# Index scores from stacked queries on the full array, in a two-block transformer program on one core

## The chip, the cores and the metric

One core of a Trainium2 chip runs the whole program in one launch. The metric is the device time of an execution in microseconds; the kernel before has a median of 1530.33 us over 3 runs (1530.08 to 1531.02).

## The reference

Two blocks of a transformer on 512 rows of width 1024, float32 throughout. The first block has three attentions side by side (a sparse one, A; a stick-breaking one, B; one over 256 memory rows, C), a gated merge and a feed-forward layer; the second block has an mLSTM layer and a dilated attention. What the change touches is the indexer of the sparse attention, which picks 128 keys for each query:

```
s     = einsum('bqhd,bkd->bqhk', iq, ik) * IDX_DIM ** -0.5     # 8 heads of 64, one shared key of 64
score = einsum('bqh,bqhk->bqk', iw, relu(s))                    # weighted sum over heads
score = where(key_chunk <= query_chunk, score, -inf)            # chunks of 64
_, idx = top_k(score, 128)
```

Queries 0 to 127 can only see 128 keys, so scores are needed for the query tiles 1 to 3 alone, against 256, 384 and 512 keys.

## The kernel before

Each engine has an instruction stream written out by hand; semaphores order them. Nearly all products run in a rounded float32 type (float32r) that loses low bits, so every operand is kept as a high part (rounded) and a low part (value less high part), and a product is made of three: high x low, low x high, high x high.

Weights come in numbered slabs of 2048 words a partition through two slots: SyncE loads a slab, ScalarE copies its high part (`split_hi`), GpSimd subtracts its low part, TensorE multiplies, and ScalarE and VectorE empty the two banks of the accumulator (PSUM) that belong to the slot.

The change lies in the stage that runs memory attention (C) in 20 steps. In each step TensorE does, in this order: the logits of one unit (head and query tile), the transposes of a unit three steps back, the output of one four steps back, then, in the steps of `SCORE_STEPS`, one score block, and last some products of weight slabs (`products_beside`, with the plan `BESIDE_C`): the two slabs of index queries `iq` in steps 0 to 4 and 5 to 12, and the first slab of `aqk` in steps 13 to 19.

A score block j (`score_pairs`: 12 of them) is a pair of heads 2p and 2p+1 and a query tile t of 1 to 3, in the order t = 1, 2, 3 for p = 0 to 3. Blocks 0 to 5 stand in steps 6 to 11, blocks 6 to 11 in steps 14 to 19. A block writes the two banks from `score_bank(j)`, which are those that the query slabs were in: blocks 0 to 5 reuse the banks of the first slab, 6 to 11 those of the second. A block waits for ScalarE and VectorE to have emptied its query slab (`ev_a`, `ev_v`) and for both ReLUs of the block before (`x_relu`).

The index queries lie transposed, two heads in one tile: head 2p on partitions 0 to 63, head 2p+1 on 64 to 127, in `iq_hi` (written by ScalarE, `index_queries`, line 1850) and `iq_low` (written by VectorE, `index_queries_low`, line 2406). The one key lies twice, on both halves, in `ik_hi` (lines 1845 and 1846) and `ik_low` (2399 and 2400). A score product uses 64 rows of the array; the two heads of a block use the two halves of it in turn.

Behind a block ScalarE takes ReLUs (`index_relus`, line 1861, one step later) and VectorE adds them up with the head weights in `masks` (`index_sums`, lines 2421 and 2424, two steps later). Behind the whole stage TensorE multiplies the other `aqk` slabs and the `av` slabs, while VectorE selects the 128 largest scores (`select`, lines 2470 and 2472), with GpSimd's masks (line 751) behind that; then attention A begins.

A step of ScalarE in this stage: ReLUs of the last step's block, a copy of transposed probabilities (1783), the exponents of this step's unit (1776), now and then the high part of an attention output (1876), then a query slab that has been finished, then the split of the next weight slab (1683). A step of VectorE: sums of the block two steps back, the minimum of this step's logits (2435), the normalisation of the last step's unit (2355), now and then the low part of an output (2359), then a finished query slab.

In the trace all matrix products have the line of the helper `mm` (842), so they are told apart by the tiles they read.

Of the kernel before, what the change touches and what calls it, by code (L numbers as in the profile page):

```python
# [19 lines left out]
F32 = mybir.dt.float32  # L20
F32R = mybir.dt.float32r
ALU = mybir.AluOpType
ACT = mybir.ActivationFunctionType
# [3 lines left out]
P = 128  # L27
S = 512
# [30 lines left out]
BASE, EV_A, EV_V, COUNT = {}, {}, {}, dict(STAGES)  # L59
# [132 lines left out]
def score_bank(j):  # L192

    return 2 if j < 6 else 0
# [32 lines left out]
def _program(nc, A, ctx):  # L227
# [3 lines left out]
    def place(name, kib, words, dtype=F32, parts=P):  # L231
        return nc.alloc_sbuf_tensor_at(name, [parts, words], dtype, offset=SB0 + int(kib * 1024))

    def arena(name, kib, words, dtype=F32, parts=P):
        return place(name, ARENA + kib, words, dtype, parts)

    def sem(name):
        return ctx.enter_context(nc.semaphore(name))
# [53 lines left out]
    cqT = arena("cqT", 0, 4 * S)  # L292
    yc_hi, yc_lo = arena("yc_hi", 0, 4 * S, F32R), arena("yc_lo", 8, 4 * S, F32R)
    mkT, mv = arena("mkT", 64, 4 * N_MEM), arena("mv", 68, 2 * HALF)
    iq_hi, iq_low = arena("iq_hi", 16, 4 * S, F32R), place("iq_low", 0, 4 * S, F32R)
    ik_hi, ik_low = arena("ik_hi", 24, S, F32R), place("ik_low", 8, S, F32R)
    relu = arena("relu", 74, 4 * S)
    iw_row = arena("iw_row", 26, S, parts=8)
    masks, work = arena("masks", 48, PACK), arena("work", 53, PACK)
# [66 lines left out]
    banks = ctx.enter_context(nc.psum_tensor("banks", [P, 8, 512], F32))  # L366
# [17 lines left out]
    ev_a, ev_v = sem("emptied_by_scalar"), sem("emptied_by_vector")  # L384
# [7 lines left out]
    x_mm, x_relu, x_acc = sem("index_mm"), sem("index_relu"), sem("index_acc")  # L392
# [26 lines left out]
    dl_gap, dl_factor = sem("dilated_gaps"), sem("dilated_factors")  # L419
    dp_norm, dp_tr, dp_copied, dp_pv = (sem(n) for n in ("dilated_scaled", "dilated_transposed", "dilated_copied", "dilated_outputs"))  # L420
    z_first, z_first_sig = sem("first_head_gate"), sem("first_head_gate_sigmoid")
    iq_lo = sem("first_index_query_lo")
    seam_lo, rows_made = sem("seam_slab_lo_piece"), sem("projected_rows_gained")
    first_lo = sem("first_slabs_lo")
    out_done = sem("out_done")
# [414 lines left out]
    def _(pe):  # L840
        def mm(out, lhsT, rhs, start, stop, **kw):
            return pe.matmul(out, lhsT, rhs, start=start, stop=stop, **kw)  # L842
# [208 lines left out]
        slot = wait_slab("ik", 0, 0, 0)  # L1051
        hi, lo = (slot_of(w, slot, KD * IK_W).rearrange("p (k c) -> p k c", k=KD) for w in (w_hi, w_lo))
        for k in range(KD):
            ins = mm3(banks[0:IK_W, 2 * slot, :], hi[:, k], lo[:, k], h_hi[:, k * S:(k + 1) * S], h_lo[:, k * S:(k + 1) * S],
                      k == 0, k == KD - 1)
# [5 lines left out]
        for step in range(16 + LAG_OUT):  # L1061
            if step < 16:
                h, t = divmod(step, 4)
                attn_logits(U_C + step, lambda u: mm(banks[:, 4 + u % 2, 0:N_MEM], cqT[:, h * S + t * P:h * S + (t + 1) * P],
                                                     mkT[:, h * N_MEM:(h + 1) * N_MEM], True, True))
            if 0 <= step - LAG_T < 16:
                u = step - LAG_T
                attn_transposes(U_C + u, prob[(U_C + u) % 4], 2)
            if step >= LAG_OUT:
                u = step - LAG_OUT  # L1070
                h, t = divmod(u, 4)
                pe.wait_ge(at_trc, U_C + u + 1)
                if u == 0:
                    pe.wait_ge(iw_made, 1)
                if t == 0 and h >= 1:
                    pe.wait_ge(at_lo, h)
                for m in range(2):
                    ins = mm(banks[:, 7, t * P:(t + 1) * P], mv[:, m * HALF + h * P:m * HALF + (h + 1) * P],
                             probT[(U_C + u) % 2][:, m * P:(m + 1) * P], m == 0, m == 1)
                ins.then_inc(at_out, 1)  # L1080
            if step == 1:
                pe.wait_ge(ev_v, EV_V["ik"] + 1)
                for t in range(NT):
                    ins = pe.transpose(banks[:, 7, 8 * t:8 * t + 8], iw_row[:, t * P:(t + 1) * P], const("ident")[0:8, 0:8])
                ins.then_inc(iw_T, 1)
            for j, pair, t in score_pairs(step):
                pe.wait_ge(ev_a, EV_A["iq"] + 1 + pair // 2)
                pe.wait_ge(ev_v, EV_V["iq"] + 1 + pair // 2)
                if j:
                    pe.wait_ge(x_relu, 2 * j)  # L1090
                for n, (queries, keys) in enumerate(((iq_low, ik_hi), (iq_hi, ik_low), (iq_hi, ik_hi))):
                    for b in range(2):
                        rows = slice(64 * b, 64 * b + 64)
                        ins = mm(banks[:, score_bank(j) + b, 0:(t + 1) * P], queries[rows, pair * S + t * P:pair * S + (t + 1) * P],
                                 keys[rows, 0:(t + 1) * P], n == 0, n == 2)
                        if n == 2:
                            ins.then_inc(x_mm, 1)
            if step == 13:
                pe.wait_ge(x_relu, 12)
            products_beside(BESIDE_C, step)  # L1100
# [137 lines left out]
        for step in range(1, 8 + 2):  # L1238
# [17 lines left out]
            if step <= 8:  # L1256
                h = step - 1
# [155 lines left out]
        for step in range(1, 4 + 1):  # L1413
# [3 lines left out]
            if step >= 1:  # L1417
                h = step - 1
# [7 lines left out]
                for t in range(NT):  # L1426
                    if h:
                        pe.wait_ge(m_h, 4 * (h - 1) + t + 1)
                    for kt in range(t + 1):
                        off = TILE_AT[kt] + (t - kt) * P  # L1430
                        ins = mm(banks[:, 4 + t, 0:V1W], wts[h % 2][:, off:off + P], v1[:, (4 * kt + h) * V1W:(4 * kt + h + 1) * V1W], kt == 0, kt == t)
# [131 lines left out]
        for pair in range(4, 16):  # L1563
# [7 lines left out]
            if pair % 2:  # L1571
                n = pair // 2 - 2
# [84 lines left out]
    def _(act):  # L1657
# [189 lines left out]

        def index_queries(i, s, j, slot):
            for b in range(2):
                ins = act.activation(iq_hi[:, (2 * s + b) * S:(2 * s + b + 1) * S], banks[:, 2 * slot + b, :], ACT.Copy)  # L1850
            ins.then_inc(ev_a, 1)

        def index_relus(step):
# [12 lines left out]
        for step in range(16 + LAG_OUT):  # L1866
# [6 lines left out]
            if (step - LAG_OUT) % 4 == 3 and step >= LAG_OUT:  # L1873
                h = (step - LAG_OUT) // 4
# [19 lines left out]
        for step in range(32 + LAG_OUT):  # L1894
# [5 lines left out]
            if (step - LAG_OUT) % 8 == 7 and step >= LAG_OUT:  # L1900
                pair = (step - LAG_OUT) // 8
# [13 lines left out]
        for step in range(8 + 2):  # L1915
# [18 lines left out]
            for n, c in enumerate((LATER, FIRST)):  # L1934
# [3 lines left out]
                if 1 <= step <= 8:  # L1938
                    h = step - 1
# [7 lines left out]
            if step >= 3 and step % 2 == 1:  # L1947
                pair = (step - 3) // 2
# [145 lines left out]
        for step in range(4 + 2):  # L2094
            if step < 4:
                h = step
# [8 lines left out]
            if step >= 2:  # L2105
                h = step - 2
                if h:
                    act.wait_ge(m_ss, h)
                for t in range(NT):
                    act.wait_ge(m_h, 4 * h + t + 1)  # L2110
                    ins = act.activation(junk[:, 256 * t:256 * t + 256], o2[:, t * D + h * 256:t * D + (h + 1) * 256], ACT.Square,
                                         accum_out=head_ss[:, 4 * h + t:4 * h + t + 1])
# [153 lines left out]
    def _(dve):  # L2266
# [106 lines left out]
        for t in range(2):  # L2373
            ins = dve.tensor_scalar(root_diag[:, t * P:(t + 1) * P], const("ident"), root_of("mem", t), None, ALU.mult)
# [5 lines left out]
        keys = mkT[:].rearrange("p (h m) -> p h m", h=4)  # L2380
# [19 lines left out]
            dve.tensor_tensor(ik_low[64:128, :], banks[0:64, 2 * slot, :], ik_hi[0:64, :].bitcast(F32), ALU.subtract).then_inc(ev_v, 1)  # L2400

        def index_queries_low(i, s, j, slot):
            dve.wait_ge(ev_a, EV_A["iq"] + s + 1)
            for b in range(2):
                c = slice((2 * s + b) * S, (2 * s + b + 1) * S)
                ins = dve.tensor_tensor(iq_low[:, c], banks[:, 2 * slot + b, :], iq_hi[:, c].bitcast(F32), ALU.subtract)
            ins.then_inc(ev_v, 1)

        def score_row(t):
# [18 lines left out]
        for step in range(16 + LAG_OUT):  # L2428
# [10 lines left out]
            if (step - LAG_OUT) % 4 == 3 and step >= LAG_OUT:  # L2439
                h = (step - LAG_OUT) // 4  # L2440
# [12 lines left out]
        for t in range(1, NT):  # L2453
            diag = masks[:, ROW_AT[t] + t * P:ROW_AT[t] + (t + 1) * P]
            ins = dve.tensor_tensor(diag, diag, const("adm"), ALU.add)
# [21 lines left out]
        for n, (stage, s, empty) in enumerate(to_empty):  # L2477
# [3 lines left out]
            if n_now == n_select:  # L2481
                dve.wait_ge(selected, n_select)
                for t in range(1, NT):
                    ins = dve.tensor_scalar(score_row(t), work[:, ROW_AT[t]:ROW_AT[t] + (t + 1) * P], TAKEN, NEG, ALU.not_equal, ALU.mult)
# [12 lines left out]
        for step in range(32 + LAG_OUT):  # L2497
            if step < 32:
                u, t = U_A + step, head_and_tile(step)[1]
# [467 lines left out]
```

## Time and profile before

| | |
|---|---|
| median of 3 runs | 1530.33 us |
| the profiled execution | 1531.11 us, span 1529.4 us |
| TensorE products | 1508.4 us busy, 7624 instructions |
| TensorE weight loads | 1252.6 us busy |
| VectorE | 701.4 us busy |
| ScalarE | 604.4 us busy |
| GpSimd | 680.5 us busy |
| granted TensorE clock | 0.999 of full speed over the span |

The span is the time between the first and the last instruction that the profiler saw; the profiled execution's own time is 1.7 us longer. Busy times of TensorE count products that overlap, so a product's cost in a stream is the distance between starts. A row of a timeline can join several instructions of one kind (x2, x4).

### The profile page before, as it was taken

How to read it: one execution, taken by the hardware profiler on the slowest of the kernel's cores; microseconds unless marked ns; L12 is line 12 of the kernel's file. 1: busy time of each engine (PE TensorE's matmuls, PEld its weight loads, DVE VectorE, ACT ScalarE, POOL GpSimd, SP SyncE). 2: the span in 40 equal slices, each digit the busy share in tenths (PEclk: the TensorE clock that was granted, in tenths of full speed). 3: DMA queues.
4: the chain of work that ended last, by engine and by line, in shares of the span. 5: the costliest groups of instructions: out<-in, count | busy, mean ns of one | idle time of the engine just before them, and what ended most of it. 6: DMA issues, size and time to landing. Idle time of an engine off the chain costs nothing.

```text
span 1529.4 us, 19806 instructions
## 1 busy us (share of the span) xinstructions
PE 1508.4 (99%) x7624; PEld 1252.6 (82%) x7624; DVE 701.4 (46%) x1183; ACT 604.4 (40%) x925; POOL 680.5 (44%) x303
## 2 busy tenths in 40 slices
PE   7999999999999999999999999999999999999998
PEld 7877966977888888888888888888888888888887
DVE  3268955483224226666655004640026237355733
ACT  5353255574233225121212114522253443447552
POOL 6323465245555535444444344443442344445332
PEclk9999999999999999999999999999999999999999
DMA  7313312433433332433332324534421222333121
GB/s 240 113 55 123 99 56 70 120 87 111 130 103 102 98 109 75 115 100 95 97 102 91 110 83 56 114 89 105 120 87 49 97 83 83 103 109 106 50 90 56
DMA packets 152646, 148.42 MB, mean 97 GB/s; under 512 B 11088, under 2 KB 121680, under 8 KB 152444
## 3 DMA queue, kind: packets, MB, share of 16 engines
q1 hardware_dynamic: 147780, 139.24, 31.5%
q10 hardware_dynamic: 4792, 8.15, 1.6%
q8 instruction: 51, 0.84, 0.2%
q14 instruction: 23, 0.19, 0.0%
HBM read 137.87 MB, written 3.21 MB: 92 GB/s over the span
## 4 chain that ended last, share of the span: by engine, by line
PE 89%; issue 3%; ACT 3%; POOL 2%; DVE 2%; DMA 1%; ACTq 0%; SPq 0%; POOLq 0%; DVEq 0%
PE banks L842 86%; PE banks L871 2%; POOL w_lo L662 1%; PE banks L1030 1%; DMA sq<-in_c_sq 1%; POOL w_lo L682 1%; PE banks L1495 0%; ACT w_hi L1683 0%; POOL stick_a L723 0%; DMA vec_rows<-in_norm_a 0%; ACT k L2170 0%; ACT stick_a L1941 0%; ACT h_hi L1763 0%; DVE head_ms L2802 0%; POOL head_rs L805 0%
## 5 line engine op out<-in xcount | busy, mean ns | idle before, releaser
L662 POOL TENSOR_TENSOR w_lo<-raw,w_hi 128x2048 fp32r<-128x2048 f32 x103 | 476.8, 4629 | 579.0 <-ACT w_hi L1683 579.0
L842 PE MATMUL banks<-h_hi,w_hi 128*128 128x512 f32 (+1 forms) x904 | 350.1, 387 | 1.5 <-DVE h_lo L2340 0.8
L842 PE MATMUL banks<-h_hi,w_lo 128*128 128x512 f32 (+1 forms) x904 | 341.0, 377 | 0.0
L842 PE MATMUL banks<-h_lo,w_hi 128*128 128x512 f32 (+1 forms) x904 | 340.8, 377 | 0.0
L1683 ACT ACTIVATE w_hi<-raw 128x2048 fp32r<-128x2048 f32 (+2 forms) x123 | 233.2, 1896 | 206.4 <-PE banks L842 202.2
L842 PEld LDWEIGHTS banks<-h_hi,w_hi 128*128 128x128 f32 x904 | 170.2, 188 | 37.9 <-issue 5.8
L842 PE MATMUL banks<-w_hi,h_hi 128*128 128x512 f32 (+1 forms) x544 | 200.0, 368 | 0.0
L842 PE MATMUL banks<-w_hi,h_lo 128*128 128x512 f32 (+1 forms) x544 | 198.5, 365 | 0.0
L842 PE MATMUL banks<-w_lo,h_hi 128*128 128x512 f32 (+1 forms) x544 | 198.4, 365 | 0.0
L842 PEld LDWEIGHTS banks<-h_hi,w_lo 128*128 128x128 f32 x904 | 169.8, 188 | 32.0
L842 PEld LDWEIGHTS banks<-h_lo,w_hi 128*128 128x128 f32 x904 | 170.2, 188 | 28.8
L682 POOL TENSOR_TENSOR w_lo<-raw,w_hi 128x512 fp32r<-128x512 f32 x88 | 118.5, 1370 | 132.0 <-ACT w_hi L1683 119.7
L842 PEld LDWEIGHTS banks<-w_hi,h_hi 128*128 128x128 f32 x544 | 102.7, 189 | 16.2 <-issue 0.6
L842 PEld LDWEIGHTS banks<-w_hi,h_lo 128*128 128x128 f32 x544 | 102.7, 189 | 16.2
L842 PEld LDWEIGHTS banks<-w_lo,h_hi 128*128 128x128 f32 x544 | 102.7, 189 | 15.9
L2639 DVE TENSOR_TENSOR f_lo<-ff_prod,f_hi 128x512 f32 x22 | 104.3, 4741 | 2.7
L2026 ACT ACTIVATE ff_sig<-banks 128x512 f32<-128x512 f32 x22 | 13.2, 599 | 175.8 <-PE banks L842 175.8
L842 PE MATMUL banks<-w_hi,f_lo 128*128 128x512 f32 x176 | 68.6, 390 | 0.0
L842 PE MATMUL banks<-w_lo,f_hi 128*128 128x512 f32 x176 | 68.6, 390 | 0.0
L842 PE MATMUL banks<-w_hi,f_hi 128*128 128x512 f32 x176 | 68.6, 390 | 0.0
L1963 ACT ACTIVATE gate<-banks,col 128x512 f32<-128x512 f32 x23 | 15.8, 689 | 125.9 <-PE banks L842 125.9
L2322 DVE TENSOR_SCALAR meansq<-sumsq 128x1 f32<-128x1 f32 (+2 forms) x16 | 3.6, 228 | 134.9 <-ACT junk L1995 130.9
(355 smaller groups left out, 2320.2 us busy)
## 6 DMA issues: line engine op xcount, KB each, us to landing
raw<-in_w_in SPq DMA_DIRECT2D x56, 512.0 KB, 3.8
raw<-in_w_ffn_in SPq DMA_DIRECT2D x44, 512.0 KB, 4.9
raw<-in_w_in_a SPq DMA_DIRECT2D x32, 512.0 KB, 5.6
raw<-in_w_ffn_out SPq DMA_DIRECT2D x22, 512.0 KB, 4.0
raw<-in_w_ple_gate SPq DMA_DIRECT2D x16, 512.0 KB, 4.8
raw<-in_w_in_b SPq DMA_DIRECT2D x16, 512.0 KB, 4.5
raw<-in_w_out SPq DMA_DIRECT2D x8, 512.0 KB, 3.6
raw<-in_w_out_a SPq DMA_DIRECT2D x8, 512.0 KB, 4.4
```

The lines of the kernel that those rows point to most:

```text
L662: pool.tensor_tensor(slot_of(w_lo, slot), slot_of(raw, slot), slot_of(w_hi, slot).bitcast(F32), ALU.subtract).then_inc(lo_made, 1)
L682: ins = pool.tensor_tensor(w_lo[:, c], raw[:, c], w_hi[:, c].bitcast(F32), ALU.subtract)
L842: return pe.matmul(out, lhsT, rhs, start=start, stop=stop, **kw)
L871: ins = pe.transpose(banks[:, transposed_bank(name, k), t * P:(t + 1) * P], rows(t)[:, k * P:(k + 1) * P], const("ident"))
L1030: ins = pe.transpose(banks[:, 6, kt * P:(kt + 1) * P], src[:, kt * P:(kt + 1) * P], const("ident"))
L1683: act.activation(slot_of(w_hi, slot, words), slot_of(raw, slot, words), ACT.Copy).then_inc(hi_made, 1)
L1963: act.activation(gate[slot][:], banks[:, 2 * slot, :] if logits is None else logits, ACT.Sigmoid, bias=col[:, ds(V_BGATE + KD * (s % 3) + ...
L2026: act.activation(ff_sig[:], banks[:, 2 * slot, :], ACT.Sigmoid).then_inc(ev_a, 1)
L2322: dve.tensor_scalar(meansq[:, c], pieces[:, :, 0], EPS, None, ALU.add).then_inc(n_ms, 1)
L2639: dve.tensor_tensor(lo, ff_prod[:], hi.bitcast(F32), ALU.subtract).then_inc(lo_ffn, 1)
```

## The change

The queries of each head are stacked on 128 partitions in one tile, `iq_stack`: for an even head the high part on partitions 0 to 63 and the low part on 64 to 127, for an odd head the high part on 64 to 127 and the low part on 0 to 63. With the key's high part (or its low part) on both halves, one product over 128 rows gives (high + low) x key part, so a score is two full-array products, with `ik_low` and with `ik_hi`, and the product low x low is now in it.

ScalarE writes the high parts in four copies of 64 partitions a slab where it had two of 128, and signals after the first two; VectorE writes the low parts, each onto the other half of the partitions, in four subtractions where it had two, and starts on the first bank at that signal. `ik_low` moves to where `iq_hi` began.

```diff
--- before.py
+++ after.py
@@ -292,8 +292,7 @@
     cqT = arena("cqT", 0, 4 * S)
     yc_hi, yc_lo = arena("yc_hi", 0, 4 * S, F32R), arena("yc_lo", 8, 4 * S, F32R)
     mkT, mv = arena("mkT", 64, 4 * N_MEM), arena("mv", 68, 2 * HALF)
-    iq_hi, iq_low = arena("iq_hi", 16, 4 * S, F32R), place("iq_low", 0, 4 * S, F32R)
-    ik_hi, ik_low = arena("ik_hi", 24, S, F32R), place("ik_low", 8, S, F32R)
+    iq_stack, ik_hi, ik_low = place("iq_stack", 0, 8 * S, F32R), arena("ik_hi", 24, S, F32R), arena("ik_low", 16, S, F32R)
     relu = arena("relu", 74, 4 * S)
     iw_row = arena("iw_row", 26, S, parts=8)
     masks, work = arena("masks", 48, PACK), arena("work", 53, PACK)
@@ -419,7 +418,7 @@
     dl_gap, dl_factor = sem("dilated_gaps"), sem("dilated_factors")
     dp_norm, dp_tr, dp_copied, dp_pv = (sem(n) for n in ("dilated_scaled", "dilated_transposed", "dilated_copied", "dilated_outputs"))
     z_first, z_first_sig = sem("first_head_gate"), sem("first_head_gate_sigmoid")
-    iq_lo = sem("first_index_query_lo")
+    iq_lo, iq_first_hi = sem("first_index_query_lo"), sem("index_queries_first_hi")
     seam_lo, rows_made = sem("seam_slab_lo_piece"), sem("projected_rows_gained")
     first_lo = sem("first_slabs_lo")
     out_done = sem("out_done")
@@ -1088,13 +1087,10 @@
                 pe.wait_ge(ev_v, EV_V["iq"] + 1 + pair // 2)
                 if j:
                     pe.wait_ge(x_relu, 2 * j)
-                for n, (queries, keys) in enumerate(((iq_low, ik_hi), (iq_hi, ik_low), (iq_hi, ik_hi))):
-                    for b in range(2):
-                        rows = slice(64 * b, 64 * b + 64)
-                        ins = mm(banks[:, score_bank(j) + b, 0:(t + 1) * P], queries[rows, pair * S + t * P:pair * S + (t + 1) * P],
-                                 keys[rows, 0:(t + 1) * P], n == 0, n == 2)
-                        if n == 2:
-                            ins.then_inc(x_mm, 1)
+                for b in range(2):
+                    queries = iq_stack[:, (2 * pair + b) * S + t * P:(2 * pair + b) * S + (t + 1) * P]
+                    mm(banks[:, score_bank(j) + b, 0:(t + 1) * P], queries, ik_low[:, 0:(t + 1) * P], True, False)
+                    mm(banks[:, score_bank(j) + b, 0:(t + 1) * P], queries, ik_hi[:, 0:(t + 1) * P], False, True).then_inc(x_mm, 1)
             if step == 13:
                 pe.wait_ge(x_relu, 12)
             products_beside(BESIDE_C, step)
@@ -1847,7 +1843,11 @@
 
         def index_queries(i, s, j, slot):
             for b in range(2):
-                ins = act.activation(iq_hi[:, (2 * s + b) * S:(2 * s + b + 1) * S], banks[:, 2 * slot + b, :], ACT.Copy)
+                for r in range(2):
+                    h, rows = 4 * s + 2 * b + r, slice(64 * r, 64 * r + 64)
+                    ins = act.activation(iq_stack[rows, h * S:(h + 1) * S], banks[rows, 2 * slot + b, :], ACT.Copy)
+                if b == 0:
+                    ins.then_inc(iq_first_hi, 1)
             ins.then_inc(ev_a, 1)
 
         def index_relus(step):
@@ -2400,10 +2400,13 @@
             dve.tensor_tensor(ik_low[64:128, :], banks[0:64, 2 * slot, :], ik_hi[0:64, :].bitcast(F32), ALU.subtract).then_inc(ev_v, 1)
 
         def index_queries_low(i, s, j, slot):
-            dve.wait_ge(ev_a, EV_A["iq"] + s + 1)
+            dve.wait_ge(iq_first_hi, s + 1)
             for b in range(2):
-                c = slice((2 * s + b) * S, (2 * s + b + 1) * S)
-                ins = dve.tensor_tensor(iq_low[:, c], banks[:, 2 * slot + b, :], iq_hi[:, c].bitcast(F32), ALU.subtract)
+                if b:
+                    dve.wait_ge(ev_a, EV_A["iq"] + s + 1)
+                for r in range(2):
+                    c, rows, other = slice((4 * s + 2 * b + r) * S, (4 * s + 2 * b + r + 1) * S), slice(64 * r, 64 * r + 64), slice(64 - 64 * r, 128 - 64 * r)
+                    ins = dve.tensor_tensor(iq_stack[other, c], banks[rows, 2 * slot + b, :], iq_stack[rows, c].bitcast(F32), ALU.subtract)
             ins.then_inc(ev_v, 1)
 
         def score_row(t):
```

## Rows read from the trace of the kernel before

**Rows 1.** The page, part 1: busy us, share of the span, instructions of each engine.
```profile
PE 1508.4 (99%) x7624; PEld 1252.6 (82%) x7624; DVE 701.4 (46%) x1183; ACT 604.4 (40%) x925; POOL 680.5 (44%) x303
```

**Rows 2.** Chain that ended last, 72 to 135 us: start us, us, what.
```profile
86.31 0.10 DVE iq_low L2406
86.92 0.69 DVE iq_low L2406
87.61 0.14 issue
```

**Rows 3.** TensorE's timeline, memory attention's steps: start us, us, line, operation [idle before].
```profile
87.75 0.39 PE L842 MATMUL banks<-ik_hi,iq_low 64*128 64x256 f32 x2 [0.49 <-DVE iq_low L2406]
...
88.64 0.40 PE L842 MATMUL banks<-h_lo,w_hi 128*128 128x512 f32 x1
...
91.06 0.44 PE L842 MATMUL banks<-ik_hi,iq_low 64*128 64x384 f32 x2
...
97.50 0.61 PE L842 MATMUL banks<-probT,mv 128*128 128x128 f32 x4
...
98.26 0.28 PE L842 MATMUL banks<-ik_low,iq_hi 64*128 64x256 f32 x2
98.38 0.28 PE L842 MATMUL banks<-ik_hi,iq_hi 64*128 64x256 f32 x2
98.58 0.51 PE L842 MATMUL banks<-h_hi,w_hi 128*128 128x512 f32 x1
98.92 0.40 PE L842 MATMUL banks<-h_lo,w_hi 128*128 128x512 f32 x1
...
104.14 0.61 PE L842 MATMUL banks<-probT,mv 128*128 128x128 f32 x4
...
105.91 0.39 PE L842 MATMUL banks<-h_lo,w_hi 128*128 128x512 f32 x1
...
107.72 0.61 PE L842 MATMUL banks<-probT,mv 128*128 128x128 f32 x4
...
108.39 0.39 PE L842 MATMUL banks<-h_lo,w_hi 128*128 128x512 f32 x1
...
113.90 0.39 PE L842 MATMUL banks<-ik_hi,iq_low 64*128 64x256 f32 x2
```

**Rows 4.** TensorE's timeline: full-array products of 512, 256 columns, and stick-breaking's stacked ones.
```profile
121.34 0.39 PE L842 MATMUL banks<-h_lo,w_hi 128*128 128x512 f32 x1
121.57 0.40 PE L842 MATMUL banks<-h_hi,w_lo 128*128 128x512 f32 x1
...
171.06 0.28 PE L842 MATMUL banks<-w_hi,h_hi 128*128 128x256 f32 x1
171.18 0.28 PE L842 MATMUL banks<-w_lo,h_hi 128*128 128x256 f32 x1
...
299.97 1.44 PE L842 MATMUL banks<-stacked 128*128 128x384 f32 x8
301.24 0.86 PE L842 MATMUL banks<-sp_hi,sums_r 128*128 128x384 f32 x6
```

**Rows 5.** ScalarE's timeline: index keys, the first query slab, block 0's ReLUs.
```profile
69.07 0.59 ACT L1845 ACTIVATE ik_hi<-banks 64x512 fp32r<-64x512 f32 x1 [2.94 <-PE banks L842]
69.67 0.59 ACT L1846 ACTIVATE ik_hi<-banks 64x512 fp32r<-64x512 f32 x1
...
85.13 1.07 ACT L1850 ACTIVATE iq_hi<-banks 128x512 fp32r<-128x512 f32 x2
...
90.28 0.64 ACT L1861 ACTIVATE relu<-banks 128x256 f32<-128x256 f32 x2
```

**Rows 6.** VectorE's timeline: low parts of the index keys and the second query slab.
```profile
70.30 0.68 DVE L2399 TENSOR_TENSOR ik_low<-banks,ik_hi 64x512 fp32r<-64x512 f32 x1 [0.54 <-ACT ik_hi L1846]
70.99 0.68 DVE L2400 TENSOR_TENSOR ik_low<-banks,ik_hi 64x512 fp32r<-64x512 f32 x1
...
112.35 1.29 DVE L2406 TENSOR_TENSOR iq_low<-banks,iq_hi 128x512 fp32r<-128x512 f32 x2 [1.27 <-ACT iq_hi L1850]
```

**Rows 7.** VectorE's timeline: the copy of the last value slab.
```profile
187.82 0.69 DVE L2292 COPY av<-banks 128x512 f32<-128x512 f32 x1 [1.79 <-PE banks L842]
```

## The prediction

> **What bounds the kernel now.** Read the page's busy times first: TensorE is busy for 1508.4 of 1529.4 us [rows 1], so a change counts only by what it does to TensorE's stream. The change lies in the stage where memory attention's 20 steps run beside the index scores, from about 84 to 132 us. The chain of waits of that stretch comes next: it stays on TensorE nearly throughout, and leaves it only for the emptying of the first index-query slab, ScalarE's high parts and then VectorE's low parts; the second low part ends at 87.61 [rows 2], and the first score product starts at 87.75, where the row names that wait, 0.49 us [rows 3]. So two things set the end here: the TensorE time of the 12 score blocks (one for a pair of heads and a query tile), and the emptying of two query slabs, which blocks 0 and 6 await. Last come the timelines of the three engines, read for starts, not busy times: products overlap, and what one costs is the distance from its start to the next.
>
> **The change part by part. The score products.** Before, a block has three products for each of two heads, on 64 rows each; a row of the trace joins the two heads (x2). With 256 keys the second and third such row start 0.12 apart (98.26, 98.38), so both heads' products pass in the time of one [rows 3]. The whole price of a block is read by comparing steps. From the step's memory-attention output to the second slab product behind it: 97.50 to 98.92 = 1.42 us with 256 keys, 104.14 to 105.91 = 1.77 with 512, and 107.72 to 108.39 = 0.67 where there is no block [rows 3]. A block costs 0.75 and 1.10, and by interpolation 0.93 with 384 keys. The 0.12 (0.23 with 512, as [rows 4] have it) three times over is only 0.36 (0.69): some 0.39 to 0.41 us of a block is fixed, at its start and its end.
>
> After, a block has four products on the full array. Full-array products of this type start 0.12 apart with 256 columns (171.06, 171.18) and 0.23 with 512 (121.34, 121.57) [rows 4]; 384 is taken as 0.176, between them. The stick-breaking stage already has this form, two products of one stationary operand in a row into one bank, in all four widths: eight of them take 299.97 to 301.24 = 1.27 us, 2560 columns [rows 4], which the figures above reproduce to 0.08. A block becomes 0.48, 0.70 or 0.93: less by 0.27, 0.22 and 0.17. Blocks 2 to 5 together (512, 256, 384, 512 keys) gain 0.83, and 8 to 11 the same. Blocks 0, 1, 6 and 7 start behind a wait (below), where the start's fixed cost is mostly hidden: block 0 takes 87.75 to 88.64 = 0.89 to the second slab product [rows 3], after 0.48 + 0.08 + 0.23 = 0.79, so I take 0.10 for blocks 0 and 6 and 0.05 for 1 and 7.
>
> The Trainium skill, in TensorEngine Tiling (Array Packing), section Key Properties, speaks against the change: row tiles run independently and in parallel, so two 64-row products cost one, and three such pairs become four. By that alone the blocks would cost 4 x (0.12 + 0.176 + 0.23) = 2.1 us more. The same list says that a change of tiling mode drains the array; the trace bears out both, and here the fixed 0.39 us is larger than the extra product.
>
> **Emptying the query slabs.** ScalarE's two copies of 128x512 become four of 64x512, VectorE's two subtractions also four. Half the partitions don't halve the time: ScalarE's 64x512 copies take 0.59 us each, VectorE's subtractions 0.68 [rows 5, 6]. Their distance matters as much. Two 128-row subtractions start 0.61 apart (86.31, 86.92) and two copies take 1.07 together, but a pair whose second writes the other half of the partitions doesn't overlap: copies 0.60 apart (69.07, 69.67), subtractions 0.69 (70.30, 70.99) [rows 2, 5, 6]. In the new order every instruction changes halves against the one before it, so I take 0.60 and 0.69. Bounds: 0.48 and 0.61 below; above, no row shows a subtraction from the upper half to the lower, and I allow it as much as double.
>
> The Trainium skill has a rule for it, in VectorE: DVE Perf Modes, section Two Vector instructions with no wait between them: an instruction whose operand or output starts in another quarter of the partitions than the last one's is held until all earlier ones have finished. By it all four are held, in both directions, and the emptying is the 0.69 case; without it, the 0.61 case below.
>
> First slab: ScalarE starts at 85.13 [rows 5], has the first half done at 86.32, VectorE starts 0.11 later (the new signal lets it go on the first half) and ends at 86.43 + 4 x 0.69 = 89.19, no longer waiting for ScalarE, which ends at 87.5. With the 0.14 of before, block 0 starts at 89.33: TensorE is 1.58 us late, 1.48 after the block. Behind the subtractions VectorE has the next step's minimum, ScalarE behind that the exponents, a weight-slab copy, and then block 0's two ReLUs, which block 1 awaits. They ended at 90.92, just before block 1's 91.06 [rows 3, 5], and now move by 1.67 (the minimum too was overlapped and isn't now): block 1 starts at 92.72, 1.66 late, 1.61 behind it. Blocks 2 to 4 bring this to 0.95, block 5 to 0.78.
>
> Second slab: what ScalarE and VectorE have in front of it hangs on TensorE's step 11 and comes 0.88 late (0.95 less 0.07 of slack). The subtractions, 112.35 to 113.64 and 0.26 before block 6 at 113.90 [rows 3, 6], become 112.35 + 0.88 + 0.12 + 2.76 = 116.11; block 6 starts at 116.26, 2.36 late, 2.26 behind it; block 7, by the same ReLU path, is 2.49 late, 2.44 behind it; blocks 8 to 11 leave **1.6 us**.
>
> **What else moves.** TensorE's other waits in these steps, for the softmax, look a step or more (3 us) back and take the delay. The next queue to mind is VectorE's top-k selection, which runs unbroken behind this stage; it had finished 1.79 us before the copy of the last value slab [rows 7], and its start moves with TensorE's step 19, by about as much as TensorE itself, so it costs nothing; beyond 1.8 us more than TensorE's shift it would. No DMA is added or moved; what lies behind waits on TensorE and moves with it. Moving the tiles' places costs nothing.
>
> **The sum**: 1529.4 + 1.6 = 1531.0 us of span, 1532.7 with the 1.7 that lie around it in the profiled run (1531.11). That run is 0.8 above the median, so for the median: 1530.33 + 1.6 = 1531.9 us.
>
> **The rivals.** (a) The emptying overlaps as 128-row instructions do (0.48, 0.61). Then block 0 is 1.22 late, block 1 1.20, block 6 1.52, block 7 1.57, the end 0.7: 1531.0. For it: the rows of two 128-row instructions; against it: both pairs of 64-row ones. (b) The emptying stays hidden and TensorE's gain stands alone: 2 x 0.83 plus 0.3 to 1.0 for the four other blocks, 1527.7 to 1528.4. That needs 64-row instructions at half the price, which rows 5 and 6 deny. (c) Slower: the fixed 0.39 us isn't the change of array shape but stays with the start of a block, where TensorE's queue has its three waits for emptied slabs and ReLUs. Then the eight free blocks cost 0.12, 0.17 and 0.22 more instead of less, 1.5 us instead of -1.7: +4.7, 1535.0. It decides from about half of the fixed cost, +3.2. For it: the gap ahead of a block stands where those waits are; against it: a gap stands behind a block too, where there is no wait (98.38 to 98.58 is 0.20 for 0.12), and the stick-breaking products follow a wait with none. Subtractions twice as long from the upper half to the lower, two in a slab, would end at about the same, +4.4.
>
> **How the numbers follow.** Forecast 58%, (a) 20%, (b) 7%, (c) with the long subtractions 10%, 5% for what I don't see. A measurement of this kernel tells 0.2% (3.1 us) from no change. Forecast, (a) and (b) lie within it, but for the far end of (b): faster 3%, same 87%, slower 10%. The range reaches from inside (b) to the point where (c) decides: 1529.5 to 1533.7.
>
> **What would show it.** Right: copies 0.60 and subtractions 0.69 apart; block 0 near 89.3 and block 6 near 116.3, both behind VectorE, blocks 1 and 7 behind ReLUs; free blocks of 0.48, 0.70 and 0.93 us; the products behind the stage some 1.6 us later than before, and that shift unchanged to the end. Wrong: a gap ahead of the free blocks, a selection that ends after the value products, or a shift that grows behind 190 us.

## The result, and the profile after

The changed kernel takes 1533.46 us (median of 22 runs, 1531.77 to 1536.54) against 1531.00 of the kernel before on the same chip (22 runs, 1530.08 to 1533.08): a ratio of 1.0017 with an interval of 1.0011 to 1.0023, 2.5 us more. Measured once more beside other kernels it was 1532.98 (11 runs) against 1531.18, 1.0014 (1.0005 to 1.0023). Both lie within the 0.2% that the prediction calls no change, but both intervals lie above 1: the kernel became a little slower. The profiled execution took 1533.76 us, with a span of 1532.0; [rows 1] read now:

```profile
PE 1509.2 (99%) x7600; PEld 1255.2 (82%) x7600; DVE 705.8 (46%) x1187; ACT 608.1 (40%) x929; POOL 680.2 (44%) x303
```

TensorE has 24 instructions fewer and is busy for 0.8 us more: the first sign that something beside the products moved. To place it, take the tile view of the kernel before, of the change, and of the change profiled a second time. The columns after the count are the shortest, median and longest duration in ns, then the first and the last start in us. In each pair of lines the first is memory attention's logits, the second those of the next attention.

```profile
L842 PE MATMUL banks<-mkT,cqT x32: 377/378/382, 68.9 to 116.2; 128*128 128x256 f32 x32
L842 PE MATMUL banks<-aqkT x64: 271/482/694, 187.7 to 261.4; 64*128 64x128 f32 x16, 64*128 64x256 f32 x16, 64*128 64x384 f32 x16, 64*128 64x512 f32 x16
```

```profile
L841 PE MATMUL banks<-mkT,cqT x32: 377/377/628, 68.5 to 119.1; 128*128 128x256 f32 x32
L841 PE MATMUL banks<-aqkT x64: 272/481/693, 190.3 to 264.0; 64*128 64x128 f32 x16, 64*128 64x256 f32 x16, 64*128 64x384 f32 x16, 64*128 64x512 f32 x16
```

```profile
L841 PE MATMUL banks<-mkT,cqT x32: 377/377/382, 69.0 to 118.5; 128*128 128x256 f32 x32
L841 PE MATMUL banks<-aqkT x64: 272/481/693, 189.7 to 263.4; 64*128 64x128 f32 x16, 64*128 64x256 f32 x16, 64*128 64x384 f32 x16, 64*128 64x512 f32 x16
```

From the first memory-attention logits to the first logits of the next attention is 118.8 us before, 121.8 after, 120.7 in the second profile. This distance, called the stage below, holds the difference: from there to the end of the span it is 1341.7 us in all three (1529.4 - 187.7, 1532.0 - 190.3, 1531.5 - 189.7 = 1341.8). What lies ahead of the stage differs between executions whatever the kernel (68.1 to 70.9 us in those below), and is left out of it. So the change costs 1.9 us in one execution and 3.0 in another.

The chain of waits after, where the kernel before has two copies [rows 5] and two subtractions [rows 2] (start, us, what; a piece in the chain can be a part of an instruction):

```profile
84.85 0.48 ACT iq_stack L1848
85.34 0.60 ACT iq_stack L1848
86.04 0.69 DVE iq_stack L2409
86.73 0.49 DVE iq_stack L2409
87.44 0.68 DVE iq_stack L2409
88.14 0.71 DVE iq_stack L2409
```

The four subtractions start 0.69, 0.71 and 0.70 apart. The four copies of the first slab in ScalarE's timeline, less one duration of 0.60, start 0.60 apart in the mean; VectorE's subtractions of the second slab end at 116.85:

```profile
84.75 2.40 ACT L1848 ACTIVATE iq_stack<-banks 64x512 fp32r<-64x512 f32 x4
114.05 2.80 DVE L2409 TENSOR_TENSOR iq_stack<-banks,iq_stack 64x512 fp32r<-64x512 f32 x4 [1.38 <-ACT iq_stack L1848]
```

TensorE's timeline of the same profile (start, duration, operation; in brackets the idle time ahead and what ended it), where [rows 3] had 87.75 and 113.90:

```profile
88.98 0.36 PE L841 MATMUL banks<-ik_low,iq_stack 128*128 128x256 f32 x1 [2.10 <-DVE iq_stack L2409]
...
89.60 0.63 PE L841 MATMUL banks<-h_hi,w_hi 128*128 128x512 f32 x1
90.03 0.63 PE L841 MATMUL banks<-h_lo,w_hi 128*128 128x512 f32 x1
...
99.74 0.61 PE L841 MATMUL banks<-probT,mv 128*128 128x128 f32 x4
...
100.89 0.40 PE L841 MATMUL banks<-h_lo,w_hi 128*128 128x512 f32 x1
...
105.89 0.61 PE L841 MATMUL banks<-probT,mv 128*128 128x128 f32 x4
...
107.49 0.39 PE L841 MATMUL banks<-h_lo,w_hi 128*128 128x512 f32 x1
...
116.94 0.36 PE L841 MATMUL banks<-ik_low,iq_stack 128*128 128x256 f32 x1 [1.38 <-issue]
...
120.43 0.41 PE L841 MATMUL banks<-ik_low,iq_stack 128*128 128x384 f32 x1 [0.31 <-ACT relu L1861]
```

Three things are to be seen. Block 0 is held 2.10 us (0.49 before), block 6 1.38; its row names no releaser, but it starts 0.09 behind the second slab's subtractions. The free blocks, those that wait for nothing, are cheaper: output to second slab product is 100.89 - 99.74 = 1.15 us with 256 keys and 107.49 - 105.89 = 1.60 with 512, where [rows 3] had 1.42 and 1.77. And behind block 0's hold the slab products start 0.43 apart and last 0.63, where the same form elsewhere starts 0.23 apart and lasts 0.39: six of them cost some 1.2 us more. The windows of the two profiles of the change say why (PE, PEld, DVE, ACT and POOL busy, granted clock, DMA share, GB/s):

```profile
89.00:93.00 4.00, 4.00 (x13) 3.21 (x14) 0.81 (x4) 2.94 (x5) 1.19 (x1) 0.57 0.00 0
```

```profile
89.00:93.00 4.00, 3.25 (x19) 2.76 (x19) 2.20 (x9) 3.14 (x7) 0.66 (x1) 1.00 0.02 4
```

In the first the granted clock fell, from its level of 2.4 GHz to 1.2, for most of these 4 us; in the second, behind a hold of the same 2.10 us, it did not. Rows of the second profile:

```profile
89.50 0.36 PE L841 MATMUL banks<-ik_low,iq_stack 128*128 128x256 f32 x1 [2.10 <-DVE iq_stack L2409]
...
90.05 0.40 PE L841 MATMUL banks<-h_hi,w_hi 128*128 128x512 f32 x1
90.29 0.40 PE L841 MATMUL banks<-h_lo,w_hi 128*128 128x512 f32 x1
...
92.95 0.41 PE L841 MATMUL banks<-ik_low,iq_stack 128*128 128x384 f32 x1 [0.25 <-ACT relu L1861]
...
116.38 0.36 PE L841 MATMUL banks<-ik_low,iq_stack 128*128 128x256 f32 x1 [1.39 <-issue]
...
119.87 0.41 PE L841 MATMUL banks<-ik_low,iq_stack 128*128 128x384 f32 x1 [0.31 <-ACT relu L1861]
```

### The profile page after: what moved, and what is told of

It reads as the page before. It is cut to its first block, busy times and chain, and to the rows that moved or that the text cites. A ratio compares the mean times of both kernels' runs of the same rounds, so it can differ in the third digit from the quotient of the medians.

```text
span 1532.0 us, 19766 instructions
## 1 busy us (share of the span) xinstructions
PE 1509.2 (99%) x7600; PEld 1255.2 (82%) x7600; DVE 705.8 (46%) x1187; ACT 608.1 (40%) x929; POOL 680.2 (44%) x303
## 4 chain that ended last, share of the span: by engine, by line
PE 89%; ACT 3%; issue 3%; POOL 2%; DVE 2%; DMA 1%; ACTq 0%; SPq 0%; POOLq 0%; DVEq 0%
PE banks L841 85%; PE banks L870 2%; POOL w_lo L661 1%; PE banks L1029 1%; DMA sq<-in_c_sq 1%; POOL w_lo L681 1%; ACT w_hi L1679 0%; PE banks L1491 0%; DVE iq_stack L2409 0%; POOL stick_a L722 0%; DMA vec_rows<-in_norm_a 0%; ACT k L2170 0%; ACT stick_a L1941 0%; ACT h_hi L1759 0%; DVE head_ms L2805 0%
## 5 line engine op out<-in xcount | busy, mean ns | idle before, releaser
L681 POOL TENSOR_TENSOR w_lo<-raw,w_hi 128x512 fp32r<-128x512 f32 x88 | 118.8, 1372 | 136.0 <-ACT w_hi L1679 123.7
```

What stands on the lines that cost most here:

```text
L681: ins = pool.tensor_tensor(w_lo[:, c], raw[:, c], w_hi[:, c].bitcast(F32), ALU.subtract)
```

## The experiments

Twelve runs, eleven of them of a new kernel, all timed in five rounds. Theory 1 is the forecast's: the products gain 2 us and the emptying of the query slabs takes more than that. Theory 3, in some expectations, is that a fall of the clock costs nothing that isn't regained. The diffs are against the change unless said otherwise, and shortened: `...`, `first`, `second` and `all 128 rows` stand for longer expressions. Each time stands with its ratio to the kernel before on the same chip.

**old_products**: the new emptying, with the old three products of 64 rows.

```diff
-                for b in range(2):
-                    mm(..., iq_stack[all 128 rows], ik_low, True, False)
-                    mm(..., iq_stack[all 128 rows], ik_hi, False, True)
+                for n, keys in enumerate((ik_hi, ik_low, ik_hi)):
+                    for b in range(2):
+                        mm(..., iq_stack[64 * b:64 * b + 64], keys[64 * b:64 * b + 64], n == 0, n == 2)
```

> The new emptying alone: eight half-partition instructions a slab, but three products of 64 rows a head as before (the low parts of the queries are written and awaited, not multiplied). Theory 1 (the emptying of the query slabs holds TensorE at blocks 0 and 6, in the profile of the change for 2.1 and 1.4 us, and behind the longer hold the granted clock falls to 0.57 for some 4 us; the full-array products themselves gain about 2 us): slower than the change by about 2 us, 1535.3, that is 4.4 us over before; holds at blocks 0 and 6 as in the change, and a stretch of about 3 us at half clock behind the first. Theory 2 (the emptying is hidden, and it is the full-array products that cost): about as before, 1531 to 1531.5.

Measured 1535.69, 1.0028 (1.0018 to 1.0039); stage 122.4. The granted clock is 1.00 throughout the stage: the fall expected behind block 0's hold didn't come in this profile.

**old_emptying**: the new products, with two copies and two subtractions of 128 partitions, and VectorE waiting for both copies as before.

```diff
-                for r in range(2):
-                    ins = act.activation(iq_stack[rows, h], banks[rows, 2 * slot + b, :], ACT.Copy)
+                ins = act.activation(iq_stack[:, first], banks[:, 2 * slot + b, :], ACT.Copy)
...
-                for r in range(2):
-                    ins = dve.tensor_tensor(iq_stack[other, c], banks[rows, ...], iq_stack[rows, c], ALU.subtract)
+                ins = dve.tensor_tensor(iq_stack[:, second], banks[:, ...], iq_stack[:, first], ALU.subtract)
```

> The new products alone: the slabs are emptied by two 128-partition copies and two 128-partition subtractions as before, into the same stack tile (so the parts lie in the wrong places of the stack and the scores are not the reference's). Theory 1: the free blocks keep 0.48, 0.70 and 0.93 us, block 0 waits about as long as before (0.5 to 0.7 us), no fall of the clock, and the time is 1.7 to 2.3 us under before: 1528.7 to 1529.3. Theory 2: still 1 to 2.5 us over before.

Measured 1529.16, 0.9987 (0.9978 to 0.9996); stage 117.2. The score blocks' waits for an emptying on TensorE's timeline, first with the old products, then with the old emptying:

```profile
91.41 0.39 PE L841 MATMUL banks<-ik_hi,iq_stack 64*128 64x256 f32 x2 [2.10 <-DVE iq_stack L2413]
119.17 0.39 PE L841 MATMUL banks<-ik_hi,iq_stack 64*128 64x256 f32 x2 [1.38 <-issue]
```

```profile
86.99 0.35 PE L841 MATMUL banks<-ik_low,iq_stack 128*128 128x256 f32 x1 [0.48 <-DVE iq_stack L2403]
```

The two halves of the change add up: in the stage +3.6 for the emptying and -1.6 for the products are +2.0, for 1.9 in the change's second profile; in the times +4.5 and -2.0 are +2.5, the measured loss (1.8 the second time). The holds of 2.10 and 1.38 come with the emptying whatever the products; 0.48 comes without it. Theory 2, in which the products cost, is out.

**products_first** and **empty_first** kept the change and tried to hide the emptying: the first by putting each step's slab products ahead of its score block on TensorE, the second by letting ScalarE and VectorE empty a finished slab at the start of a step, ahead of its softmax work.

```diff
+            products_beside(BESIDE_C, step)
             for j, pair, t in score_pairs(step):
                 ...
-            products_beside(BESIDE_C, step)
```

> The change, but in each step of TensorE the weight-slab products stand ahead of the score block, so that 1.4 us of other work lie between the step's start and the block. Theory 1: the hold at block 0 falls from 2.1 to about 0.8 us, that at block 6 to 0.2 or less, the clock stays at 1.0, and the time is about 1.4 + 1.4 + 1.2 us under the change: 1529.5, 1.5 under before. Without the clock's part (theory 3: the fall of the clock costs nothing that isn't regained) 1530.7. Theory 2: as the change, 1533.5.

> The change, but ScalarE and VectorE empty a finished query slab at the start of their step, ahead of the softmax work of the step, 1.3 us earlier. Theory 1: the hold at block 0 falls to about 0.9 us, that at block 6 to about 0.2, the clock stays at 1.0, and the time comes to 1529.7 (between 1529.2 and 1530.4). Theory 3: 1530.9. Theory 2: as the change, 1533.5.

Measured 1532.88, 1.0012 (1.0003 to 1.0021), and 1535.15, 1.0025 (1.0016 to 1.0034): both far above the 1529.5 and 1529.7 expected (stages 120.9 and 122.6). The holds at blocks 0 and 6 shrank as expected; new ones came. Of products_first:

```profile
88.55 0.36 PE L841 MATMUL banks<-ik_low,iq_stack 128*128 128x256 f32 x1 [0.71 <-DVE iq_stack L2409]
120.10 0.68 PE L841 MATMUL banks<-probT,mv 128*128 128x128 f32 x4 [0.82 <-DVE yc_lo L2359]
133.11 0.47 PE L841 MATMUL banks<-h_hi,w_hi 128*128 128x512 f32 x1 [1.36 <-ACT relu L1861]
```

The last is block 11, which now ends step 19: nothing stands between its ReLUs and the next slab that awaits them. Of empty_first, TensorE and then ScalarE:

```profile
87.44 0.35 PE L841 MATMUL banks<-ik_low,iq_stack 128*128 128x256 f32 x1 [0.41 <-DVE iq_stack L2416]
91.80 0.41 PE L841 MATMUL banks<-ik_low,iq_stack 128*128 128x384 f32 x1 [1.17 <-ACT relu L1866]
119.75 0.66 PE L841 MATMUL banks<-ik_low,iq_stack 128*128 128x384 f32 x1 [2.02 <-ACT relu L1866]
```

```profile
87.79 0.51 ACT L1772 ACTIVATE prob<-prob,negmax 128x256 f32<-128x256 f32 x1 [1.76 <-DVE prob L2446]
...
89.22 1.90 ACT L1679 ACTIVATE w_hi<-raw 128x2048 fp32r<-128x2048 f32 x1
91.02 0.64 ACT L1866 ACTIVATE relu<-banks 128x256 f32<-128x256 f32 x2
```

ScalarE waits for the softmax minimum, which VectorE makes behind the subtractions; behind the exponents it copies a weight slab (1.90 us), and only then come block 0's ReLUs, which block 1 awaits. So the simple form of theory 1 (hide the one wait and the gain is there) fell: what is late is a row of work on two engines.

**early_slabs** makes the room on TensorE's side: each query slab is finished one step earlier, the blocks stay. **before_early_slabs** is the kernel before with the same edit, and its diff is against that.

```diff
-BESIDE_C = [("iq", 0, 0, 5), ("iq", 1, 5, 8), ("aqk", 0, 13, 7)]
+BESIDE_C = [("iq", 0, 0, 4), ("iq", 1, 4, 8), ("aqk", 0, 12, 8)]
...
-            if step == 13:
+            if step == 12:
                 pe.wait_ge(x_relu, 12)
```

> The change, with the products of the first index-query slab in steps 0 to 3 (before 0 to 4), of the second in 4 to 11 (before 5 to 12) and of the next slab in 12 to 19 (before 13 to 19), so that each query slab is emptied one step earlier and the score blocks stay where they are. Theory 1 (the loss is the emptying that TensorE awaits at blocks 0 and 6, and ScalarE's softmax work queued behind it): about 4.8 us of TensorE work now cover an emptying of 4.1, the next slab's 1.9 us copy of weights no longer stands ahead of block 0's ReLUs, both holds go and so do the waits for ReLUs of blocks 1 and 7; the stage is 116.5 us long (118.8 in the kernel before, 121.8 in the change), the time 1528.8, no fall of the granted clock. Theory 2 (the products cost more than they gain): the stage stays above 118.8 and the time above 1531. A new wait may come at step 12, where the next slab's products await block 5's ReLUs behind only 2.1 us of work: at most 1 us.

> The kernel before with the same earlier query slabs. Theory 1: it loses its own holds of 0.5 and some tenths at the blocks 0 and 6, stage 118.1, time 1530.4; so the change is worth 1.6 us under this order, from its products alone. Theory 2: it is as fast as or faster than the change in this order.

Measured 1532.88, 1.0013 (1.0004 to 1.0022), and 1530.60, 0.9998 (0.9989 to 1.0007). In early_slabs (stage 121.1) blocks 0 and 6 wait no more, as expected, but the time missed by 4 us; in this order the kernel before is the faster one, as theory 2 had it, though not by its reason. Before_early_slabs has a stage of 118.8, as without the edit, where 118.1 was expected: block 0's 0.49 is gone, but the step of block 7 is 0.42 longer, 0.18 of it a wait for a ReLU. TensorE and ScalarE of early_slabs around step 14:

```profile
117.47 0.41 PE L1029 MATMUL banks<-sq,prob 128*128 128x128 f32 x2 [2.09 <-ACT probT L1779]
```

```profile
114.66 0.51 ACT L1772 ACTIVATE prob<-prob,negmax 128x256 f32<-128x256 f32 x1 [3.40 <-DVE prob L2438]
...
115.17 1.89 ACT L1679 ACTIVATE w_hi<-raw 128x2048 fp32r<-128x2048 f32 x1
116.97 0.36 ACT L1779 ACTIVATE probT<-banks 128x256 f32<-128x256 f32 x1
```

It is the same row of work, with the weight copy now ahead of a softmax copy that TensorE awaits; and the granted clock was 0.57 from 118 to 122 us.

**halves_together** is the change with both copies, and both subtractions, of one half of the partitions next to each other, and **after_again** the change once more.

```diff
-            for b in range(2):
-                for r in range(2):
+            for r in range(2):
+                for b in range(2):
```

> The change, with the four copies and the four subtractions of an emptying in another order: both of one half of the partitions, then both of the other, so that only the middle one of the three steps changes halves. If what keeps 64-row instructions apart is the change of halves, the subtractions start 0.61, 0.70, 0.61 apart and the copies 0.53, 0.60, 0.53; an emptying ends about 0.2 us earlier and the time falls by 0.3 to 0.4. If 64-row instructions are kept apart whatever the halves, the distances stay 0.70 and 0.60 and the time doesn't move.

> The change as it is, profiled once more. Theory 1: the hold of 2.10 us ahead of block 0 comes again. If the half clock behind it belongs to such a hold, 89 to 93 us shows a granted clock near 0.57 again and the stage is 121.8 us; if it comes only in some executions, the clock is 1.00, the stage about 120.5, and the times of this kernel spread by 1 us or more, as those without the hold don't.

Measured 1532.08, 1.0007 (0.9998 to 1.0016), and the 1532.98 given above: 0.9 less for the order of the halves, where 0.3 to 0.4 was expected. Halves_together on VectorE and TensorE:

```profile
85.99 2.59 DVE L2409 TENSOR_TENSOR iq_stack<-banks,iq_stack 64x512 fp32r<-64x512 f32 x4 [1.26 <-ACT iq_stack L1848]
```

```profile
88.73 0.36 PE L841 MATMUL banks<-ik_low,iq_stack 128*128 128x256 f32 x1 [1.78 <-DVE iq_stack L2409]
```

The four subtractions take 2.59 us where they took 2.80: less one duration of 0.68 they start 0.64 apart in the mean, for 0.70. So the change of halves is what kept them apart. The hold is 0.32 shorter, block 6's too (1.06), and the stage, 120.0, by about their sum, 0.7. After_again answered the clock's question: it falls in some executions only. Theory 3 is out: the fall made the stage 1.1 us longer, and what follows took 1341.7 and 1341.8 with and without it.

**early_slabs_late_split** moves ScalarE's weight copy to one step later, and **early_late_halves** adds the order of halves_together to that.

```diff
+            late = 1 if slabs is BESIDE_C and step > 2 else 0
-            for stage, s in slabs_begun(slabs, step):
+            for stage, s in slabs_begun(slabs, step - late):
                 split_hi(0, stage, s)
```

> The change with the query slabs one step earlier, as the last kernel of that kind, and ScalarE's copy of the next weight slab (1.9 us) one step later, where the kernel before has it. Theory 1 (what is late is no single wait but the row of work on ScalarE and VectorE behind an emptying): the holds of 0.52 and 2.09 us ahead of the transposes, which stood behind that copy, fall to 0.2 or less, no fall of the granted clock, stage 117.5 us, time 1529.5 to 1530, below the kernel before. Rival (the row of work is too long wherever it stands): the copy stands ahead of block 0's ReLUs again, blocks 1 and 7 wait 0.5 us or more, stage 119 or more, time 1531 or more.

> The same, with the copies and subtractions of one half of the partitions together. Theory 1: an emptying is 0.3 us shorter, which counts only if something still waits behind it; 1529.3 to 1530. Rival: 0.3 to 0.6 below the kernel without it and still 1531 or more.

Measured 1533.63, 1.0017 (1.0008 to 1.0026), and 1532.54, 1.0010 (1.0001 to 1.0019), with stages of 121.4 and 120.9: the rival's case. The copy stood ahead of the ReLUs again; blocks 1 and 7 waited 1.05 and 2.02 us in the first, 0.73 and 2.03 in the second.

**subtract_twice** is the change with every pair of subtractions made twice (`for n in range(2)` around them, VectorE waiting for the first pair).

> The change with each pair of low-part subtractions made twice, 2.8 us more of VectorE work in an emptying and nothing else. Theory 1 (TensorE awaits the emptying in full): block 0 is held 4.9 us where it was 2.10, block 6 4.2 to 4.5 where it was 1.38; stage 126.5 us without a fall of the granted clock, up to 2.2 more if it falls behind both, time 1538.9 to 1541. Theory 2 (the emptying lies partly beside other work and the loss is the products'): the time rises by less than 4 us. The clock: if a fall belongs to a hold that is long enough, both holds show it here.

Measured 1540.92, 1.0065 (1.0051 to 1.0079), stage 128.6. The two holds, and the windows behind them:

```profile
93.83 0.35 PE L842 MATMUL banks<-ik_low,iq_stack 128*128 128x256 f32 x1 [4.95 <-DVE iq_stack L2411]
124.63 0.35 PE L842 MATMUL banks<-ik_low,iq_stack 128*128 128x256 f32 x1 [4.24 <-issue]
```

```profile
94.00:97.00 3.00, 3.00 (x10) 2.48 (x10) 0.67 (x4) 2.81 (x5) 0.34 (x1) 0.54 0.00 0
125.00:128.00 3.00, 3.00 (x10) 2.42 (x10) 0.52 (x2) 2.94 (x5) 0.49 (x1) 0.50 0.02 5
```

Each hold grew by 2.85 us, and VectorE's subtractions of a slab take 5.64 where they took 2.80: TensorE pays for the emptying one to one. The stage grew by 7.9 over the 120.7 of the change's second profile: 5.7 of holds, and 2.2 that are left for the fall of the granted clock behind each.

**copy_after_relus** is early_late_halves with `late = 3` (from step 5 on), so that the weight copy stands behind block 0's and block 1's ReLUs.

> The last kernel (query slabs one step earlier, halves together) with ScalarE's copy of the next weight slab two steps later still, in steps 8 and 16, so that it stands behind block 0's and block 1's ReLUs (6's and 7's), not ahead of them. Theory 1: with a slab finished three steps before its first block the emptying itself is covered, and what was left of the loss is that 1.9 us copy, which waits for VectorE's minimum behind the emptying and holds block 0's and block 6's ReLUs; blocks 1 and 7 then wait 0.3 us or less where they waited 0.73 and 2.03, no fall of the granted clock, stage 117 to 117.8 us, time 1529 to 1530, below both kernels. Rival (ScalarE has too much in these steps, wherever the copy stands): blocks 2 and 8 wait in their place, 0.5 us or more each, stage 119 or more, time 1531 or more.

Measured 1528.89 (1528.08 to 1529.48), 0.9985 (0.9976 to 0.9994); stage 116.7. TensorE's one wait at a score block, and ScalarE:

```profile
115.51 0.41 PE L841 MATMUL banks<-ik_low,iq_stack 128*128 128x384 f32 x1 [0.22 <-ACT relu L1862]
```

```profile
88.90 0.64 ACT L1862 ACTIVATE relu<-banks 128x256 f32<-128x256 f32 x2
...
91.60 0.87 ACT L1862 ACTIVATE relu<-banks 128x384 f32<-128x384 f32 x2
...
94.31 1.91 ACT L1679 ACTIVATE w_hi<-raw 128x2048 fp32r<-128x2048 f32 x1
```

The granted clock is 1.00 throughout the stage. The time is below both kernels and just below the 1529 expected: 2.0 us less than the one before on its chip. Against before_early_slabs, which has the products of before with no wait for an emptying left, its stage is 2.1 us shorter (116.7 for 118.8): about what the new products are worth once the emptying is out of the way. These two were not timed side by side, and differ in the order of the halves and the place of the weight copy too; both still wait some 0.2 us at block 7. The weight copy moved behind the ReLUs alone, with the slabs finished as late as in the change, was not run.

## Why the prediction was right or wrong

The forecast was 1531.9 in a range of 1529.5 to 1533.7, with 87% on no change; 1533.46 lies inside, near its slow end, and the verdict is the likeliest one. That it lies inside is in part luck: the slow end of the range was set by rival (c), which did not come (by its own +3.2 it would decide at 1533.5, not 1533.7); what took the time there is a first median that was 0.67 low and a term that the sum lacked, the granted clock (below). It stood on a median of three runs, 1530.33, and 22 runs gave 1531.00; like for like, +1.6 was forecast and +2.5 (1.8 the second time) measured.

- The products: right. Free blocks of 0.48 and 0.93 (1.15 and 1.60 less the 0.67 of a step without a block); the gain of about 2 us is 1.6 in the stage of old_emptying, 2.0 in its time, 2.1 in copy_after_relus. Rival (c), the fixed 0.39 us staying with the block, is refuted by the same rows. The rule of the Trainium skill (TensorEngine Tiling (Array Packing), section Key Properties) that row tiles run in parallel would have made them 2.1 us dearer, by the prediction's estimate; measured, the old form with its fixed cost is the dearer one, by 4.5 - 2.5 = 2.0 in the times.
- The emptying: right. Copies 0.60 and subtractions 0.70 apart (0.60 and 0.69 forecast), also from the upper half to the lower, so rival (a) and the long subtractions fall. Halves_together bears out the rule of the Trainium skill (VectorE: DVE Perf Modes, section Two Vector instructions with no wait between them): without the change of halves 64-row subtractions draw together, 2.80 to 2.59.
- Lateness of the blocks, from the second profile less 0.1 for its later start: block 0 1.65 (1.58 forecast), block 1 1.79 (1.66), block 6 2.38 (2.36), block 7, at 117.14 before, 2.63 (2.49). The stage, +1.9 for +1.6, is off by 0.3, some 0.12 of it at block 7's ReLUs.
- The selection's slack: right, and to 0.01. Its wait ahead of the value copy, 1.79 in [rows 7], is now

```profile
190.37 0.69 DVE L2292 COPY av<-banks 128x512 f32<-128x512 f32 x1 [1.80 <-PE banks L841]
```

- The term that the sum lacked: the granted clock. The forecast took a us of hold as a us of time. In the first profile the slab products behind block 0 ran at the low clock, 1.1 us more (121.8 for 120.7), and with that the shift is +3.0. The median lies between the two. Each execution's mean granted clock is on record, and goes with the times: of the first 22, thirteen show 0.998 or less and took 1533.21 us or more (median 1533.98), nine show 0.999 or more and took 1532.96 or less (median 1532.21, 1.2 over the kernel before); of the second 11, two show 0.998, and they are the slowest. That fits a first median that lies farther from the forecast's +1.6 than the second.
- "Wrong" had listed a gap ahead of free blocks, a selection that ends late and a shift that grows behind 190 us; none came.

Open: why the clock falls behind a hold in one execution and not in another. In how many it falls is not settled by its mean either, which is recorded to three decimals: empty_first's profile has a fall and reads 0.999. And the two groups above lie 1.8 us apart, more than the 1.1 of one fall; what else is in that is not shown.

## What to carry to other kernels

When a change makes TensorE's work cheaper and its preparation dearer, price the preparation first: here 3.6 us of the stage against 1.6. To hide it, follow the whole row of work that queues behind it on each engine in order; three re-orderings that moved only the wait in front brought it back elsewhere, two that moved an uninvolved 1.9 us copy by one step did no better, and one that moved it behind the ReLUs that TensorE awaits, as well as the rest, turned 2.5 us of loss into 2.0 of gain.

## What had not been expected of the hardware

Behind a hold of TensorE the granted clock can fall to its lower level while work is waiting, and then some 3 us of products run at half speed. Profile by profile: behind 2.10 us it fell in the change (0.57 from 89 to 93 us) but not in after_again or old_products; it fell behind 2.09 in early_slabs, behind holds of 2.02 and 2.03 in empty_first, early_slabs_late_split and early_late_halves, and behind both holds of subtract_twice, 4.95 and 4.24. It showed no fall behind the holds of 1.78 and 1.06 in halves_together. A fall cost 1.1 us between the two profiles of the change, and what is left over in subtract_twice is 2.2 for two.
